# Difference attention: projecting each head's queries and keys inside the head loop, with one pool of seven PSUM banks

## What is computed

```python
def diff_mixer(h, cos, sin, w_in, lam_p, subln_g, w_out, layer):
    q, k, v = jnp.split(h @ w_in, [DIFF_QK_W, 2 * DIFF_QK_W], axis=-1)
    q = apply_partial_rope(q.reshape(B, T, 2 * DIFF_HEADS, HEAD_DIM), cos, sin).reshape(B, T, DIFF_HEADS, 2, HEAD_DIM)
    k = apply_partial_rope(k.reshape(B, T, 2 * DIFF_HEADS, HEAD_DIM), cos, sin).reshape(B, T, DIFF_HEADS, 2, HEAD_DIM)
    v = v.reshape(B, T, DIFF_HEADS, 2 * HEAD_DIM)
    lam = jnp.exp(jnp.sum(lp[0] * lp[1])) - jnp.exp(jnp.sum(lp[2] * lp[3])) + lam_init
    o = diff_attention(q[..., 0, :], q[..., 1, :], k[..., 0, :], k[..., 1, :], v, lam)
    o = rms_norm_2(o, subln_g) * (1.0 - lam_init)
    return o.reshape(B, T, DIFF_V_W) @ w_out
```

## Time and profile before

| what | value |
|---|---|
| median of three runs | 2382.69 us |
| profiled execution, its span (first to last instruction) | 2384.1 us |
| TensorE busy in it | 2205.8 us, 93% |
| granted TensorE clock, mean | 0.964 |
| difference attention, from tile 3's projection to the output projection | 1669.08 to 1863.39 us, 194.3 us |
| of it the head loop, from the first products | 1743.68 to 1863.39 us |

### The profile page before, as it was taken

The page is one execution under the profiler, slowest core; times in us unless marked ns, Lnnn a source line. Parts: engine busy times, 40 slices in busy tenths (PEclk is TensorE's granted clock), DMA queues, the critical chain, the costliest instruction groups (busy, mean ns, idle before and its releaser), DMA issues.

```text
span 2384.1 us, 29845 instructions
## 1 busy us (share of the span) xinstructions
PE 2205.8 (93%) x10776; PEld 1785.1 (75%) x10776; DVE 1237.1 (52%) x2214; ACT 1116.8 (47%) x1958; POOL 717.4 (30%) x475
## 2 busy tenths in 40 slices
PE   7888899989999999988978999998988888999997
PEld 5655688767888887766857888887877767788886
DVE  6768544547999824455455322224567455323233
ACT  5455733456888725555353322224666334322221
POOL 4160223420000222510333323234742424333223
PEclk9879999999999999988999999999999989999999
DMA  4301032315999720220221233222311221323231
GB/s 163 115 19 36 15 106 97 115 71 196 396 392 386 280 89 19 71 97 1 74 68 57 93 107 96 98 92 67 102 58 36 71 71 40 102 97 98 97 98 53
DMA packets 71649, 258.85 MB, mean 109 GB/s; under 512 B 7952, under 2 KB 8080, under 8 KB 71120
## 3 DMA queue, kind: packets, MB, share of 16 engines
q1 hardware_dynamic: 66816, 238.76, 28.6%
q0 software_dynamic: 2816, 11.82, 1.3%
q10 hardware_dynamic: 1872, 6.37, 0.7%
HBM read 245.36 MB, written 11.56 MB: 108 GB/s over the span
## 4 chain that ended last, share of the span: by engine, by line
PE 79%; DVE 8%; ACT 6%; issue 3%; POOL 2%; DMA 1%; POOLq 0%; DVEq 0%; SPq 0%; ACTq 0%
PE ps L506 16%; PE ps L507 16%; PE ps L508 16%; PE ps L1133 3%; PE ps L566 2%; PE ps L2701 2%; PE ps L2703 2%; PE ps L2702 2%; PE ps L1148 2%; PE ps L542 2%; PE ps L548 2%; PE ps L543 2%; PE ps L1167 2%; PE ps L2728 1%; PE ps L2729 1%
## 5 line engine op out<-in xcount | busy, mean ns | idle before, releaser
L448 ACT ACTIVATE wh<-raw 128x1024 fp32r<-128x1024 f32 x308 | 322.3, 1054 | 454.0 <-PE ps L508 426.8
L453 DVE TENSOR_TENSOR wl<-raw,wh 128x1024 fp32r<-128x1024 f32 x180 | 245.4, 1369 | 532.7 <-ACT wh L448 525.0
L506 PE MATMUL ps<-hh,wh 128*128 128x512 f32 (+1 forms) x1192 | 468.4, 393 | 5.9 <-POOL wl L453 5.6
L507 PE MATMUL ps<-hl,wh 128*128 128x512 f32 (+1 forms) x1192 | 465.7, 391 | 0.0
L508 PE MATMUL ps<-hh,wl 128*128 128x512 f32 (+1 forms) x1192 | 465.4, 390 | 0.0
L453 POOL TENSOR_TENSOR wl<-raw,wh 128x1024 fp32r<-128x1024 f32 x128 | 309.3, 2417 | 473.7 <-ACT wh L448 464.5
L506 PE MATMUL ps<-act,wh 128*128 128x512 f32 (+1 forms) x688 | 270.8, 394 | 11.3 <-ACT act L1408 9.9
L507 PE MATMUL ps<-act,wh 128*128 128x512 f32 (+1 forms) x688 | 268.9, 391 | 0.0
L508 PE MATMUL ps<-act,wl 128*128 128x512 f32 (+1 forms) x688 | 268.6, 390 | 0.0
L506 PEld LDWEIGHTS ps<-hh,wh 128*128 128x128 f32 (+1 forms) x1192 | 224.5, 188 | 54.9 <-issue 7.9
L508 PEld LDWEIGHTS ps<-hh,wl 128*128 128x128 f32 (+1 forms) x1192 | 224.4, 188 | 47.7
(11 more groups left out here) (463 smaller groups left out, 3885.0 us busy)
## 6 DMA issues: line engine op xcount, KB each, us to landing
raw<-d_w SPq DMA_DIRECT2D x277, 512.0 KB, 3.7
raw_x<-d_moe SPq DMA_DIRECT2D x84, 512.0 KB, 6.3
raw<-d_moe SPq DMA_DIRECT2D x84, 512.0 KB, 6.5
d_xs<-Sb POOLq DMA_DIRECT2D x7, 514.0 KB, 7.3
Xb<-d_xs ACTq DMA_DIRECT2D x6, 514.0 KB, 5.5
area<-d_mem POOLq DMA_DIRECT2D x3, 1024.0 KB, 5.1
d_ys<-rows ACTq DMA_DIRECT2D x6, 512.0 KB, 6.0
xT<-d_x SPq DMA_DIRECT2D x8, 256.0 KB, 6.6
```

Of the source, the lines that this page charges most:

```text
L448: me.e.activation(hi, raw, ACT.Copy).then_inc(*me.done("wh", m))
L453: me.e.tensor_tensor(lo, raw, hi.bitcast(F32), ALU.subtract).then_inc(*me.done("wl", m))
L506: me.e.matmul(bank[0:m, 0:n], wh[:, c], hi, start=k == 0, stop=False)
L507: me.e.matmul(bank[0:m, 0:n], wh[:, c], lo, start=False, stop=False)
```

## The change

Queries and keys of a head now stand next to each other in the order of tiles (tile 2n the queries, 2n + 1 the keys of head n). PE projects tiles 0 to 2 together, tile 3, spreads the norm, makes head 0's value, and begins head 0's products; tile 4 follows. In step n (1 to 6) it makes products n, tile 2n + 3, the output part of head n - 1 (turning, value turning, features of head n - 2, value products), value n and tile 2n + 4 (the last tile is 15, in step 6). Step 7 has products 7, value 7 and the output of head 6; then follow the output of head 7 and its features. The steps of `heads_act`, `heads_dve` and `heads_pool` are likewise spread over the heads. DVE works out the lambda ahead of the first tile's scaling. `turns` is gone: all seven banks rotate together. The second softmax of odd heads writes to pieces of `sel`, since `tab` now has to last. Nothing is computed that was not before, and nothing less.

```diff
-    K.i_dqk = [item(spread_cols(128 * c, 128 * c + 128), a[:, c, :], rope=4, war=war) for c in range(16)]
+    K.i_dqk = [item(spread_cols(128 * c, 128 * c + 128), a[:, c, :], rope=4, war=war) for n in range(8) for c in (n, 8 + n)]
...
-    K.first = [K.S[:, 0, :, :], K.O[:, :, :]]
-    K.other = [K.S[:, 1, :, :], K.tab[:, :, :]]
+    K.first = [[K.S[:, 0, i, :] for i in range(NQ)], [K.O[:, i, :] for i in range(NQ)]]
+    K.other = [[K.S[:, 1, i, :] for i in range(NQ)],
+               [K.sel[:, 1, 384:512], K.sel[:, 2, 0:256], K.sel[:, 1, 0:384], K.sel[:, 0, :]]]
...
-        bank = K.banks[me.take("turns", "T", "diff", n, pk)]
+        bank = K.banks[me.take("ps", "T", "diff", n, pk)]
...
-    return [("comb2", n - 2)] if n >= 2 else [("end", "pe", (("ffn", 0), 2)), ("tok", "dqk", 15)]
+    return [("comb2", n - 2)] if n >= 2 else [("end", "pe", (("ffn", 0), 2))]
...
+def diff_tile_pe(K, me, t):
+    linear(K, me, ("L", "dqk", t), "od_w_in_2", 0, K.i_dqk[t]["cols"], K.h("n6"), after=[("xh", "dqk", t)])
+
+
+def diff_output_pe(K, me, m):
+
+    diff_turn_pe(K, me, m, K.i_diff[m], K.first[m % 2], ("comb2", m))
+    values_turn_pe(K, me, "vd", K.i_vd, m, NQ)
+    if m:
+        diff_features_pe(K, me, m - 1)
+    diff_values_pe(K, me, m)
 
 
 def diff_pe(K, me):
-    h = K.h("n6")
-    heads_pe(K, me, "dqk", "od_w_in_2", h, K.i_dqk, "n6", 3)
-    me.set_apart("ps", "turns", 2)
-    diff_products_pe(K, me, 0, K.i_diff[0])
+    linear_group(K, me, [(("L", "dqk", t), "od_w_in_2", 0, K.i_dqk[t]["cols"], 128) for t in range(3)], K.h("n6"), "n6")
+    for t in range(3):
+        me.give("ps", ("L", "dqk", t), ("xh", "dqk", t))
+    last_squares_pe(K, me, "n6")
+    diff_tile_pe(K, me, 3)
+    norm_spread_pe(K, me, "n6")
     diff_value_pe(K, me, 0)
-    for n in range(10):
-        if n + 1 < 8:
-            diff_products_pe(K, me, n + 1, K.i_diff[n + 1])
-        if 1 <= n < 9:
-            diff_turn_pe(K, me, n - 1, K.i_diff[n - 1], K.first[(n - 1) % 2], ("comb2", n - 1))
-        if n < 8:
-            values_turn_pe(K, me, "vd", K.i_vd, n, NQ, pool="turns")
-        if 1 <= n < 9:
-            diff_values_pe(K, me, n - 1)
-        if n >= 2:
-            diff_features_pe(K, me, n - 2)
-        if n + 1 < 8:
-            diff_value_pe(K, me, n + 1)
-    me.put_back("ps", "turns")
+    for n in range(8):
+        diff_products_pe(K, me, n, K.i_diff[n])
+        if 1 <= n < 7:
+            diff_tile_pe(K, me, 2 * n + 3)
+        if n == 7:
+            diff_value_pe(K, me, n)
+        if n:
+            diff_output_pe(K, me, n - 1)
+        if 1 <= n < 7:
+            diff_value_pe(K, me, n)
+        if n < 6:
+            diff_tile_pe(K, me, 2 * n + 4)
     me.alias("hfree", "n7")
+    diff_output_pe(K, me, 7)
+    diff_features_pe(K, me, 7)
...
 def diff_act(K, me):
-    heads_act(K, me, "dqk", K.i_dqk, "n6", 3)
+    def exps(n, part):
+        S, free = ((K.first, first_free), (K.other, second_free))[part]
+        diff_exp_act(K, me, n, K.i_diff[n], S[n % 2], free(n), part)
+
+    ahead(K, me, ("L", "dqk", 2))
+    norm_act(K, me, "n6")
+    ahead(K, me, ("L", "dqk", 3))
     ahead(K, me, ("L", "vd", 0))
     me.wait_ge("lambda", "lsum")
     me.e.activation(K.mis[:, 4:6], K.mis[:, 0:2], ACT.Exp).then_inc(*me.done("lambda", "lexp"))
-    for n in range(11):
-        if 2 <= n < 10:
-            diff_squares_act(K, me, n - 2)
+    for t in range(3):
+        swap_act(K, me, "dqk", t)
+    ahead(K, me, ("L", "dqk", 4))
+    exps(0, 0)
+    swap_act(K, me, "dqk", 3)
+    values_copy_act(K, me, "vd", K.i_vd, 0, NQ)
+    exps(0, 1)
+    for n in range(1, 10):
+        if n < 7:
+            ahead(K, me, ("L", "dqk", 2 * n + 3))
+            swap_act(K, me, "dqk", 2 * n + 2)
         if n < 8:
-            diff_exp_act(K, me, n, K.i_diff[n], K.first[n % 2], first_free(n), 0)
+            exps(n, 0)
+            ahead(K, me, ("L", "vd", n))
+        if n < 9:
+            diff_turned_copy(K, me, n - 1, K.i_diff[n - 1], pt_free("diff", n - 1, first_free(0)))
+        if n < 8:
+            exps(n, 1)
+        if n >= 2:
+            diff_hi_act(K, me, n - 2)
+        if n < 9:
+            diff_squares_act(K, me, n - 1)
+        if n < 7:
+            swap_act(K, me, "dqk", 2 * n + 3)
+        if n < 6:
+            ahead(K, me, ("L", "dqk", 2 * n + 4))
+        if n < 8:
             values_copy_act(K, me, "vd", K.i_vd, n, NQ)
-            if n + 1 < 8:
-                ahead(K, me, ("L", "vd", n + 1))
-            diff_exp_act(K, me, n, K.i_diff[n], K.other[n % 2], second_free(n), 1)
-        if 1 <= n < 9:
-            diff_turned_copy(K, me, n - 1, K.i_diff[n - 1], pt_free("diff", n - 1, first_free(0)))
-        if n >= 3:
-            m = n - 3
-            hi_act(K, me, ("dt", m), K.act[:, m, :], K.tdn("gained", m), ("gained", m), ("S", "diff", m, 1, 2))
...
+def diff_scaled_by_norm_dve(K, me, t):
+    i = me.take("td", "xh", "dqk", t)
+    me.wait_ge("L", "dqk", t)
+    me.wait_ge("R", "n6")
+    me.e.tensor_tensor(K.td[:, i, :], K.bank("L", "dqk", t), K.R[:, :], ALU.mult).then_inc(*me.done("xh", "dqk", t))
+    me.give("td", ("xh", "dqk", t), ("cosine", "dqk", t), ("swap", "dqk", t))
+
+
 def diff_dve(K, me):
-    heads_dve(K, me, "dqk", K.i_dqk, "n6", 3)
+    def maxima(n, part):
+        S, free = ((K.first, first_free), (K.other, second_free))[part]
+        diff_max_dve(K, me, n, K.i_diff[n], S[n % 2], free(n), part)
+
+    ahead(K, me, ("L", "dqk", 2))
+    norm_dve(K, me, "n6")
+    ahead(K, me, ("L", "dqk", 3))
     ahead(K, me, ("L", "vd", 0))
     diff_lambda_dve(K, me)
-    for n in range(11):
+    diff_scaled_by_norm_dve(K, me, 0)
+    diff_scaled_by_norm_dve(K, me, 1)
+    swap_dve(K, me, "dqk", 0, 4)
+    diff_scaled_by_norm_dve(K, me, 2)
+    swap_dve(K, me, "dqk", 1, 4)
+    ahead(K, me, ("L", "dqk", 4))
+    diff_scaled_by_norm_dve(K, me, 3)
+    maxima(0, 0)
+    swap_dve(K, me, "dqk", 2, 4)
+    maxima(0, 1)
+    swap_dve(K, me, "dqk", 3, 4)
+    diff_combine_dve(K, me, 0)
+    for n in range(1, 10):
+        if n < 7:
+            ahead(K, me, ("L", "dqk", 2 * n + 3))
+            diff_scaled_by_norm_dve(K, me, 2 * n + 2)
         if n < 8:
-            diff_max_dve(K, me, n, K.i_diff[n], K.first[n % 2], first_free(n), 0)
-            diff_max_dve(K, me, n, K.i_diff[n], K.other[n % 2], second_free(n), 1)
-        if 1 <= n < 9:
-            diff_combine_dve(K, me, n - 1)
-        if n >= 3:
-            diff_gained_dve(K, me, n - 3)
-        if 2 <= n < 10:
-            diff_scaled_dve(K, me, n - 2)
-        if n + 1 < 8:
-            ahead(K, me, ("L", "vd", n + 1))
-        if 1 <= n < 9:
+            maxima(n, 0)
+        if n < 7:
+            swap_dve(K, me, "dqk", 2 * n + 2, 4)
+        if n < 8:
+            maxima(n, 1)
+        if n < 7:
+            diff_scaled_by_norm_dve(K, me, 2 * n + 3)
+        if n < 8:
+            ahead(K, me, ("L", "vd", n))
+        if n < 9:
             diff_turned_copy(K, me, n - 1, K.i_diff[n - 1], pt_free("diff", n - 1, first_free(0)))
+            values_out_dve(K, me, "vd", K.i_vd, n - 1, NQ, "n6")
+        if n >= 2:
+            diff_gained_dve(K, me, n - 2)
         if n < 8:
-            values_out_dve(K, me, "vd", K.i_vd, n, NQ, "n6")
+            diff_combine_dve(K, me, n)
+        if n < 9:
+            diff_scaled_dve(K, me, n - 1)
+        if n < 7:
+            swap_dve(K, me, "dqk", 2 * n + 3, 4)
+        if n < 6:
+            ahead(K, me, ("L", "dqk", 2 * n + 4))
...
 def diff_pool(K, me):
-    heads_pool(K, me, "dqk", K.i_dqk)
+    def turned_sum(t):
+        swap_pool(K, me, "dqk", t, K.i_dqk[t]["dst"], 4, K.i_dqk[t]["war"])
+
+    ahead(K, me, ("L", "dqk", 3))
     ahead(K, me, ("L", "vd", 0))
-    for n in range(11):
-        if 2 <= n < 10:
-            diff_root_pool(K, me, n - 2)
-        if n >= 3:
-            m = n - 3
-            lo_of(K, me, ("dt", m), K.act[:, m, :], K.act[:, 8 + m, :], K.tdn("gained", m))
-        if n + 1 < 8:
-            ahead(K, me, ("L", "vd", n + 1))
+    for t in range(3):
+        turned_sum(t)
+    ahead(K, me, ("L", "dqk", 4))
+    turned_sum(3)
+    for n in range(1, 10):
+        if n < 7:
+            ahead(K, me, ("L", "dqk", 2 * n + 3))
+            turned_sum(2 * n + 2)
+        if n < 8:
+            ahead(K, me, ("L", "vd", n))
+        if n >= 2:
+            lo_of(K, me, ("dt", n - 2), K.act[:, n - 2, :], K.act[:, 6 + n, :], K.tdn("gained", n - 2))
+        if n < 9:
+            diff_root_pool(K, me, n - 1)
+        if n < 7:
+            turned_sum(2 * n + 3)
+        if n < 6:
+            ahead(K, me, ("L", "dqk", 2 * n + 4))
```

More of the change, by code:

```diff
@@ L3501, in diff_tables @@
         it = dict(width=lambda i: 128 * (i + 1), mask=K.tri, scale=64 ** -0.5, nkey=NQ, causal=True,
-                  tok=[("tok", "dqk", n), ("tok", "dqk", 8 + n)], v=lambda j, n=n: vd[:, j, 128 * n:128 * n + 128],
+                  tok=[("tok", "dqk", 2 * n), ("tok", "dqk", 2 * n + 1)], v=lambda j, n=n: vd[:, j, 128 * n:128 * n + 128],
```

(19 more changed lines are left out.)

4 lines of the change are left out of this document (2 added, 2 removed).

## The result

The changed kernel takes **2394.26 us**, the median of 5 runs (2391.69 to 2402.79); beside them the kernel before took 2383.06 (5 runs). The ratio is 1.0049, with a 95% interval of 1.0030 to 1.0068: slower, by 11.2 us in the medians. The profiled execution is the run of 2394.26, with a span of 2392.4 us.

The account below looks back on a forecast made before the run. PE, busy 93% of the span, was taken to bound the kernel. The terms summed to 201.5 us against 194.3, 7.2 slower: 2391.3 for the profiled execution, 2390 from the median, range 2379 to 2403.

Parts of the forecast that it names:

- stage: On PE, from the start of tile 3's projection to the start of the output projection: 201.5 us forecast against 194.3.
- first wait: PE waits before products 0 for tiles 0 and 1, behind DVE's split and lambda: 7.9 us, bounds 3.3 and 9.5.
- products 0 and tile 4: PE's work right behind its wait for tiles 0 and 1, at the lowered clock: 9.7 us.
- second wait: PE waits before products 1 for tile 3, which ACT swaps only after head 0's exponentials: 2.3 us.
- step 1: From products 1, with a 3.7 us wait for `val` 0 and 1.2 for the clock: 28.0 us.
- steps 2 to 5: Four loop steps of 23.5 us PE work each, plus 0.8 on average waiting for the value: 97.2 us.
- the end: From the start of products 7 to the output projection: 26.0 us, of which PE works 17.2.
- the sentence on banks: With seven banks rotating no reader comes late, so the wait before the third transposes goes: 9 us.
- The chain to the tiles: From `R`, through split, lambda, scaling, swaps, multiplying and adding, until tiles 0 and 1 are ready: PE waits 7.9 us.
- VectorE becomes the bound: Rival, chance 0.12: in six steps one more POOL split of 2.4 us delays DVE ahead of `val`, 14 us, 2404.
- Faster: Rival, chance 0.12: the start is short and VectorE keeps up; 8.7 us faster, 2374.
- It doesn't do what it says: Rival without its own chance, counted in the others: the bank wait stays where the next bank's reader is late.

Follow-up runs that it names:

- e10: The changed kernel run once more without any edit: 2399.58 us, 1.0074 of the kernel before.
- e1: The changed kernel with DVE scaling tile 3 before the weight split that stood ahead of it: 2396.46 us, 1.0045 of the kernel before.
- e6: The changed kernel with DVE's weight split for the value tile behind the value's own steps: 2396.08 us, 1.0052 of the kernel before.
- e3: The changed kernel with e1's edit, and DVE scaling tiles 0 and 1 before its weight split and the lambda: 2394.73 us, 1.0042 of the kernel before.
- e9: The changed kernel with edits of e3 and e6, tile 4 projected before products 0, later tiles one place sooner, DVE and ACT reordered: 2382.57 us, 0.9998 of before.
- e7: The kernel before, with ACT copying the transposed banks out before its second exponentials: 2376.66 us, 0.9962 of the unedited kernel.

## Why the prediction was right, and where it was not

Slower was forecast, with 2390 us and 7.2 us over the execution before. Measured were 2394.26, 8.3 us over in the profile's span and 11.2 in the medians. The sign and the mechanism hold: the twelve projections covered the start of the loop, and the waits at the banks, which were won, are worth less. The size does not. The stage was to be 7.2 us longer and is 16.3 longer, 19.2 in e10. The profile's total came as near to the forecast as it did by luck, with 8.0 us given back outside the stage; in e10 the medians are 17.4 apart. Term by term, forecast against measured:

| part | forecast | measured |
|---|---|---|
| tile 3 and spread | 5.9 | 5.9 |
| value 0 | 5.6 | 5.7 |
| first wait | 7.9 | 11.65 |
| products 0 and tile 4 | 9.7 | 10.4 |
| second wait | 2.3 | 3.2 |
| step 1 | 28.0 | 29.6 |
| steps 2 to 5 | 97.2 | 97.7 |
| step 6 | 18.95 | 20.0 |
| the end | 26.0 | 26.5 |
| stage | 201.5 | 210.6 |

**The step that failed is the sentence on banks**: "A bank that is asked for was handed out seven takes earlier, and a step has 13 takes, so its reader is more than ten us back; I found none that comes late." From step 2 on it holds: the rows of after have no such wait there. In step 1 it fails by a little, since the last transposes of head 0 wait for a bank that DVE's maxima of head 1 give back, 0.27 us in after and 1.93 in e10. And it was not applied to the start. There the reader of tile 3's bank is DVE's scaling, which stands behind the split that waits for ACT's swaps; PE asks for that bank with products 0. The first wait was mis-sized by 3.75 us, and went past the upper bound of 9.5. e1 shows 3.3 of it. The chain to the tiles was right to 0.3 us (1683.80 is 8.2 behind the start of the wait, 7.9 were forecast), with two terms whose errors nearly cancel: the lambda took 3.4 (1671.88 to 1675.31) and the split 1.1 (its start to the lambda's), where 2.1 was taken for each. That the sum came out so close is luck.

The other terms were right in kind and a little low. Behind the longer wait all of products 0 ran slow, 4.64 us where the cold ones of before, 3.52, were taken, with a granted clock of 0.77 up to the end of tile 4. Over step 1 it was 0.88, where two groups ran slow, products 1 (3.31) and the values (4.13). `val` was 2.92 late in step 1, not 3.7, and 0.35 and 1.64 in the steps behind, where 0.3 and 1.3 stood. Step 6 is 1.0 longer, which is tile 15's wait, 1.55 where 0.5 was taken. Two readings of before were off without weight in the sum: the wait of about 1.0 stands in six heads, not seven, with 2.11 in head 6, so that 8.4 us were to be won there and not 9; and eight heads of 6.8 are 54.4, not 54.8.

**The rivals.** *VectorE becomes the bound* did not happen. Steps 2 to 5 came within 0.5 us of the sum, and e6 takes the waits away by order alone. The engines do meet. In the first wait of e3 DVE's split took 2.33 where 1.22 is the shortest seen. By the Trainium skill (SBUF — State Buffer, section "Who interferes with whom") a DVE step with two SBUF inputs and a GpSimd one that reads SBUF shut each other out; for single steps the traces agree (DVE's step of 2.42 ended at 1674.30, POOL's split of 3.23 at 1674.22), and in after every one of steps 2 to 5 has such meetings, a combine of 2.86 to 2.96 in place of 1.94, a four-column step of 0.99 in place of 0.17 or 1.36 in place of 0.22, a sine step of 1.15 in place of 0.69: 1.6 to 2.3 us of DVE's time in each. They did not hold PE up: most stand behind `val` in DVE's order, and the 0.99 of steps 3 and 5, which stands ahead of it, is still there in e6 (0.98 and 0.99), where PE waits only 0.35. So the rival had the meetings right and their place wrong. *Faster*, by a short start, was tried from the other end by e3 (first wait 5.2) and e9 (none): 203.9 and 193.7 us of stage. Without its first wait the changed order just reaches the kernel before, so this rival lacked not only a short start but cover for DVE's first chain as well. *It doesn't do what it says* falls by the row at 1787.21.

**Where the expected gain was.** The waits at the transposes were real, and e7 shortened the stage by 5.9 us without a bank: ACT emptied the bank late because its copy stood behind the exponentials. The forecast named that copy as the reader, but took the seven banks as the cure and priced no other.

What stays open: why the totals of e3 and e6 do not show the 6.7 and 5.5 us by which their stages are shorter than after's. The spread of their runs (2384.9 to 2406.3 in e3) is wider than that, and after's own two medians differ by 5.3. In the profile of e3 the account closes: its stage began 9.1 us later than after's, and the part behind it is as long (517.7 and 517.8). For the 1,660 us upstream, where equal code began this stage up to 12.7 us apart, the clock is the likeliest cause: of e3's ten runs the shortest has a mean granted clock of 0.969 and the longest 0.959. No run tries it.

## What to carry to other kernels

Work that stands ahead of a loop may be cover for the loop's first chain: before it is spread into the loop, add up what DVE, ACT and POOL have to do until the first dependent matmul, and what PE has left to do meanwhile. With a bank pool in rotation, go through the first takes one by one, since "seven takes back is long ago" held here from step 2 on only. And where an engine waits for a buffer, look first at what stands before the reader in its own queue: moving ACT's copy ahead of an exponential pass won 0.38%, where the rearrangement for the same wait lost 0.49%.
